# Input-gate products in four column groups, and modulation sums by transposes and a reduce

## The reference, cut to what matters

```
proj = xn @ w_in                          # (256, 1024) @ (1024, ...)
qk, v, o, i_pre, f_pre, u, sv, gates = split(proj)   # i_pre, f_pre: 4 columns each
i_pre + b_i, f_pre + b_f                  # input and forget gates of the 4 mLSTM heads
logf = log_sigmoid(f_pre); b = cumsum(logf); ...     # stabilised chunkwise mLSTM

ada   = silu(c)     @ w_ada + b_ada       # c, c_ctx: (1, 1024), w_ada: (1024, 6144)
ada_c = silu(c_ctx) @ w_ada + b_ada
sh1, sc1, g1, sh2, sc2, g2 = split(ada)   # shift, scale and gate vectors of 1024 each
```

## Time and profile before

| what | us |
|---|---|
| median of the timed runs | 1326.96 |
| lowest and highest of the three | 1324.94, 1327.00 |
| profiled execution, whole | 1323.78 |
| its span in the trace | 1322.1 |
| TensorE busy in it | 1289.8 |
| VectorE, ScalarE busy | 695.4, 501.6 |

### The profile page before, as it was taken

How to read it: one execution, slowest core, us unless ns; L and a number is a source line. 1 busy time by engine, 2 the same in 40 slices (tenths; PEclk the granted TensorE clock), 3 DMA queues, 4 the chain that set the end, 5 groups by cost and what they waited for, 6 DMA issues and landing times.

```text
span 1322.1 us, 18062 instructions
## 1 busy us (share of the span) xinstructions
PE 1289.8 (98%) x7214; PEld 908.7 (69%) x7214; DVE 695.4 (53%) x1174; ACT 501.6 (38%) x766; POOL 77.3 (6%) x83
## 2 busy tenths in 40 slices
PE   8999999999999999999999999999999999999998
PEld 7988887976775445444445444459956687799986
DVE  5675668666565222222322222257876877755552
ACT  5555574345242211111111111146414685744442
POOL 5740200100000000000000000000000000000000
PEclk9999999999999999999999999999999999999999
DMA  9653747958865999999999999995505334655540
GB/s 350 229 191 135 254 144 260 368 194 303 308 232 199 396 424 427 427 427 428 428 428 428 427 425 428 427 397 181 180 12 196 139 129 157 195 166 183 192 159 32
DMA packets 101349, 363.68 MB, mean 275 GB/s; under 512 B 4002, under 2 KB 28837, under 8 KB 88912
## 3 DMA queue, kind: packets, MB, share of 16 engines
q1 hardware_dynamic: 97792, 352.86, 68.7%
q0 software_dynamic: 3280, 9.58, 2.2%
q10 hardware_dynamic: 192, 0.06, 0.0%
HBM read 361.43 MB, written 1.05 MB: 274 GB/s over the span
## 4 chain that ended last, share of the span: by engine, by line
PE 84%; DVE 7%; ACT 4%; DMA 2%; issue 2%; ACTq 0%; DVEq 0%
PE bank L510 37%; PE bank L908 15%; PE bank L926 9%; PE bank L883 5%; PE bank L1253 5%; PE bank L939 2%; DVE ring_parts L1301 2%; DMA ring<-in_w 2%; PE bank L835 1%; PE bank L1056 1%; PE bank L916 1%; ACT ring_parts L2119 1%; PE bank L564 1%; DMA ring<-in_w_xkv 1%; PE bank L600 1%
## 5 line engine op out<-in xcount | busy, mean ns | idle before, releaser
L2119 ACT ACTIVATE ring_parts<-ring 128x1024 fp32r<-128x1024 f32 x234 | 242.6, 1057 | 231.5 <-PE bank L510 204.2
L1301 DVE TENSOR_TENSOR ring_parts<-ring,ring_parts 128x1024 fp32r<-128x1024 f32 x214 | 257.3, 1223 | 133.1 <-ACT ring_parts L2119 130.1
L510 PE MATMUL bank<-ring_parts,arena_parts 128*128 128x512 f32 x1056 | 271.7, 392 | 3.6 <-ACT ring_parts L2119 1.5
L510 PEld LDWEIGHTS bank<-ring_parts,arena_parts 128*128 128x128 f32 x1056 | 196.4, 188 | 48.7 <-ACT ring_parts L2119 2.9
L510 PE MATMUL bank<-arena_parts,ring_parts 128*128 128x256 f32 x1504 | 198.0, 284 | 1.2 <-DVE flank_parts L1307 0.7
L909 PE MATMUL bank<-ring,arena 128*64 128x512 f32 x448 | 197.9, 594 | 0.0
L908 PE MATMUL bank<-ring,arena 128*64 128x512 f32 x432 | 190.7, 594 | 6.1 <-issue 6.1
L510 PEld LDWEIGHTS bank<-arena_parts,ring_parts 128*128 128x128 f32 x1504 | 190.1, 192 | 2.1 <-DVE flank_parts L1307 0.8
L908 PEld LDWEIGHTS bank<-ring,arena 128*64 128x64 f32 x432 | 57.4, 137 | 125.3 <-issue 125.3
L510 PE MATMUL bank<-ring_parts 128*128 128x512 f32 (+1 forms) x624 | 117.2, 346 | 2.1 <-DVE ring_parts L1301 1.2
L926 PE MATMUL bank<-ring,arena 128*64 128x512 f32 x448 | 113.4, 595 | 1.1 <-DMA ring<-in_w 1.1
(11 more groups left out here) (385 smaller groups left out, 1440.0 us busy)
## 6 DMA issues: line engine op xcount, KB each, us to landing
ring<-in_w SPq DMA_DIRECT2D x83, 2048.0 KB, 20.4
ring<-in_w_in SPq DMA_DIRECT2D x27, 2048.0 KB, 9.4
flank<-in_w SPq DMA_DIRECT2D x13, 2048.0 KB, 20.7
ring<-in_w_ada SPq DMA_DIRECT2D x12, 2048.0 KB, 8.0
ring<-in_w_ffn_gate SPq DMA_DIRECT2D x11, 1024.0 KB, 5.4
ring<-in_w_ffn_up SPq DMA_DIRECT2D x11, 1024.0 KB, 8.0
ring<-in_w_ffn_down SPq DMA_DIRECT2D x5, 2048.0 KB, 7.9
ring<-in_w_xkv SPq DMA_DIRECT2D x4, 2048.0 KB, 16.3
```

The costliest lines, as they stand in the source:

```text
L510: mm = pe.matmul(ps[:, o:o + width], *pair, start=(o == 0 and kk == 0 and ha + hw == 0), stop=(kk == kn - 1 and (ha, hw) == terms[-1] and ...
L1301: dve.tensor_tensor(low, src, high, ALU.subtract).then_inc(low_ready, 1)
L2119: act.activation(high, src, ACT.Copy).then_inc(high_ready, 1)
```

## The change

Three edits are made, and what each engine issues changes as follows.

1. `iftok` has the weights as stationary operand: `wif` is padded with zeros from 8 to 32 columns, and contraction slice k goes to column group k % 4 with all 256 tokens streaming. That is 8 products [32 x 256] instead of 16 [128 x 8]. ScalarE copies [128, 256] instead of [128, 16]. A new memset on GpSimd writes the zeros before the transfer of `wif`.
2. `if` is two products of 4 columns of `pick` (now [128, 8]) with the copied parts, 256 columns each, instead of four transposes. They add the four parts and bring the rows to partitions 0 to 3.
3. `ada_sum` for the eight j that fill `adaT` turns the parts with four transposes [128 x 128]. VectorE then sums, in place of the product with `pick`, the four columns of each output in a reduce out of PSUM (L1463 after), followed by the bias addition from `adaT`. The sums of j = 4, 5, 10 and 11 stay.

```diff
-        wif = sb("wif", [P, KD, 2 * H])
+        wif = sb("wif", [P, KD, 32])
-        pick = sb("pick", [P, 2])
+        pick = sb("pick", [P, 2 * H])
+        if_parts = work[:, 384:384 + N]
...
                 if j == 0:
                     pe.wait_ge(s["silu_c"], 2)
-                    pe.wait_ge(s["pick_ready"], 1)
...
                     for c in range(4):
-                        mm = pe.matmul(ps[:, 2 * c:2 * c + 2], parts[:, c * P:(c + 1) * P], pick[:], start=True, stop=True)
+                        mm = pe.transpose(ps[:, c * P:(c + 1) * P], parts[:, c * P:(c + 1) * P], ident[:])
...
                     ps = take("iftok")
-                    for t in range(NT):
-                        for k in range(KD):
-                            mm = pe.matmul(ps[:, t * 2 * H:(t + 1) * 2 * H], actT[:, k, t * P:(t + 1) * P], wif[:, k, :],
-                                           start=(k == 0), stop=(k == KD - 1))
+                    pe.wait_ge(s["if_zeros"], 1)
+                    for k in range(KD):
+                        g = k % 4
+                        mm = pe.matmul(ps[32 * g:32 * g + 32, 0:N], wif[:, k, :], actT[:, k, :], start=(k < 4), stop=(k >= 4),
+                                       skip_group_check=True)
...
                     ps = take("if")
+                    pe.wait_ge(s["pick_ready"], 1)
                     for g in range(2):
-                        for t in range(NT):
-                            mm = pe.transpose(ps[0:H, g * N + t * P:g * N + (t + 1) * P],
-                                              stat[:, 8 + t * 2 * H + g * H:8 + t * 2 * H + (g + 1) * H], ident[:])
+                        mm = pe.matmul(ps[0:H, g * N:(g + 1) * N], pick[:, g * H:(g + 1) * H], if_parts, start=True, stop=True)
...
-                    did(dve.tensor_tensor(adaT[:, o:o + 4, :], ps[:, 0:8].rearrange("p (c n) -> p c n", n=2),
+                    did(dve.tensor_reduce(adaT[:, o:o + 4, :], ps[:].rearrange("p (c g r) -> p c r g", c=4, g=4)[:, :, 0:2, :], AX_X, ALU.add))
+                    did(dve.tensor_tensor(adaT[:, o:o + 4, :], adaT[:, o:o + 4, :],
                                           col2("b_ada_2")[:, b0:b0 + 4].unsqueeze(2).broadcast_to([P, 4, 2]), ALU.add), free(name))
...
-            did(act.activation(stat[:, 8:24], ps[:, 0:16], ACT.Copy), free("iftok"))
+            did(act.activation(if_parts, ps[:, 0:N], ACT.Copy), free("iftok"))
...
+            pool.memset(wif[:, :, 2 * H:], 0.0).then_inc(s["if_zeros"], 1)
-            pool.dma_start(wif[:], w["w_in"][0][:, 4096:4096 + 2 * H].rearrange("(k p) n -> p k n", p=P)).then_inc(s["misc_in"], 16)
+            pool.dma_start(wif[:, :, 0:2 * H], w["w_in"][0][:, 4096:4096 + 2 * H].rearrange("(k p) n -> p k n", p=P)).then_inc(s["misc_in"], 16)
```

More of the change, by code:

```diff
@@ L337, in two_blocks @@
         for name in ("E_ready G_ready O_rms On_ready SVn_ready Y_ready Z_ready a_ready choice_ready "
-                     "comb2_ready comb_ready consts count_ready gmoe_in ctx_in decay_cols dexp dmax down filt_arg "
+                     "comb2_ready comb_ready consts count_ready if_zeros gmoe_in ctx_in decay_cols dexp dmax down filt_arg "
                      "filt_in squared hid_ones fw3_in filt_sin gate_rows hF_ready h_rms if_ready lam_dot lam_exp lam_in mem_in "
@@ L1354, in _ @@
             dve.wait_ge(s["consts"], 9)
-            did(dve.tensor_reduce(pick[:], ident[:].rearrange("p (g r) -> p r g", g=4)[:, 0:2, :], AX_X, ALU.add), s["pick_ready"])
+            did(dve.tensor_reduce(pick[:], ident[:].rearrange("p (g r) -> p r g", g=4)[:, 0:2 * H, :], AX_X, ALU.add), s["pick_ready"])
             for t in range(NT):
```

## The result

The changed kernel took 1331.14 us (median of 7 runs, 1329.56 to 1331.85) against 1326.76 us for the kernel before on the same chip, a ratio of 1.0029 with an interval of 1.0018 to 1.0041. It is slower by 0.3%, where 1324.6 us was forecast, and outside the range. One of the seven runs of the kernel before took 2641.63 us and is not in the ratio; without it its median is 1326.11 us. The profiled execution took 1331.85 us with a span of 1330.1 us, 8.0 us above the span of the earlier trace rows.

What follows compares the result with a forecast made beforehand. The prediction took TensorE, busy 1289.8 of 1322.1 us, as the main bound, with VectorE or transfers pacing some stretches. Terms of -2.48, +0.42 and -0.34 gave -2.40, so 1326.96 became 1324.56 us; range 1321.8 to 1327.3.

Steps and rivals of the forecast that it cites:

- Gate product: Product for iftok between the third unit and its predecessors: 0.99 us in place of 3.47, term -2.48 (-2.54 to -1.62).
- gate turn: Behind the gate product, two float32 products replace four transposes: 0.86 us in place of 0.44, term +0.42 (0 to +0.64).
- sum 3: Modulation sum between xkv0 and the TensorE stretch behind it: 0.45 us in place of 0.79, term -0.34 (-0.35 to -0.20).
- Rival C: Column groups of the gate product don't overlap at 256 columns: +2.7 us, 1329.7 us; chance 0.07.
- The terms at nothing: Sums 0, 1, 2, 6 and 7 to 9, VectorE's reduces, ScalarE's copy, GpSimd's memset and the waits: each term 0.
- Sums 0 to 2 and 6: Sums ahead of the memory keys and xq0: savings covered by the transfer and VectorE, term 0.
- Rival A: All sums pay: seven more give 0.34 us each, -2.38 more, 1322.2 us; chance 0.10.
- No stall for a copy: Behind the gates, copies keep up with TensorE's 2.06 us lead; GpSimd's last quarter is ready 3.1 us early.
- rival B: Behind the gates, TensorE catches up with the copies and loses 2.06 us; -0.34 left, 1326.6 us; chance 0.13.
- Each such stretch begins with a TensorE event, so it moves along: Later stretches of ScalarE, VectorE and transfers in the chain shift with TensorE, so the 2.06 us gate lead lasts.
- three signs of being wrong: Gate product over 1.9 us; low-part wait between 40 and 90 us; experts' last transfer not moving by the front's gain.
- Sum: -2.48 + 0.42 - 0.34 = -2.40 us: Whole kernel: gate product, turn and one modulation sum added, other terms 0; bounds -3.0 and -1.2.

Runs made afterwards that it cites:

- e9: Kernel before with the new modulation sums alone, plus 64 padding instructions putting the jump back at its old place; 1327.00 us, ratio 0.9995 [0.9982, 1.0008].
- e5: Changed kernel with 133 fewer never-run instructions in the part the jump skips; 1323.63 us, ratio 0.9971.
- e6: Changed kernel with 96 padding instructions (two waits each) between long products of the value units; 1323.28 us against 1327.80, ratio 0.9968.
- e12: Changed kernel with 96 padding instructions between the value units' products, run a second time; 1321.65 us, ratio 0.9953.
- e10: Kernel before, unchanged, run once more for another profile; 1326.61 us in one run.
- e1: Changed kernel with some 96 more wait instructions at the start of TensorE's program, jump back at its old place; 1328.65 us, ratio 1.0018.

## Why the prediction was wrong

**Gate product, gate turn, sum 3: right.** The terms were 0.99, 0.86 and 0.45 us, and the chain after has 1.00, 0.96 and 0.44. The turn's 0.10 too little is all that was mis-sized among them; it lies inside the bounds. Rival C (column groups that don't overlap) fell with the 1.00 us: 16 rows at 0.06 each.

**The terms at nothing: right.** Sums 0 to 2 and 6 became idle time ahead of the transfer's and VectorE's end, the heads gained nothing, and the reduces' 0.19 us lay under cover. Rival A is refuted by the idle rows; e9's interval excludes it only just. Which of VectorE's rows ends the wait ahead of `xq0` stays open: the profile names L1307 before and after, the prediction took L1342. On the rule of the Trainium skill on transposes ("TensorE: Matmul & The Clock Gate", Part 4: PE-mode transpose) the measurement stands: four take 0.44 us, not the 1.10 estimated from that page.

**No stall for a copy: right.** The units behind the gates run nearly as before (L511 at 63.34 for 21.95 us), so rival B fell too. Of the 1.95 us that the gates gave, 1.54 were left at 86 us: the gate product started 0.13 us later than before, and the units behind it took 0.09 us more (96 rows) and 0.19 more (192 rows).

**"Each such stretch begins with a TensorE event, so it moves along": half right.** The lead was 1.67 us at the keys and 1.96 at 666 us. In the profile after it was lost between 666 us and the jump, on the wait and the clock at 675 us and on the last transfer, and in e5 at 850 us; in e6 and e12 it was there at the end, with spans of 1319.8 and 1319.5 us. The last expert transfer took 20.37 to 22.06 us in the chains that show it, so a single profile can't tell a lead of 2 us from its scatter. Of the prediction's three signs of being wrong the last one came: that transfer began 1.40 us earlier and ended 0.20 later. It isn't what cost the 8 us.

**"Sum: -2.48 + 0.42 - 0.34 = -2.40 us": the failed step.** The sum took only what the changed instructions do in their own places. It was right for them: without the stall the forecast span was 1319.7 us, and e6 and e12 measured 1319.8 and 1319.5 (e5, with its own late wait, 1323.4).
**The median.** The forecast put the same shift on the median. As it stands the change costs 4.4 us; with the jump repaired it gave more than forecast, 4.5 us in e6 and 7.1 in e12. That the rest is the clock's fall behind the old product, which the first profile of before lacked and e10's had, fits the count of profiles above, but no run shows how often the timed executions had it.

## What to carry to other kernels

Count where each taken jump and its target lie in the engine's instruction stream, before and after an edit, whenever code is skipped: 333 skipped instructions stalled or didn't by their place alone, 200 didn't where 333 did, and by the rule that fits all runs up to 256 never can (only the 200 was run). If a change leaves its own lines as forecast and the time moves elsewhere, look for a wait whose releaser is "issue" and put padding or a shorter jump against it before judging the change. "issue" alone is no proof: it stands at seven waits of L908 in each of the two kernels as well, and at 675 us one ended on a transfer. What marks a jump to missing code is the record of the jump itself (6.28 us in place of 0.48) and the block of instructions that moves only behind it. A few per mille between two versions of one kernel may be such a placement, so compare them with their jumps in the same place.

## What the runs showed of the hardware

- A jump to code that isn't fetched left TensorE idle for 5.76 to 5.88 us in four kernels with busy DMA queues and for 3.13 us with quiet ones. The granted clock was at half in or behind it, and the 48 rows that followed took 12.81 to 13.93 us in the four, in place of 11.17.
- 96 instructions that do nothing but wait (e1, e6) cost 5.6 us at the start of the program and nothing between 128 x 512 products.
- The clock can be at half behind a stretch in which TensorE was never idle by its rows: 32 rows of 8 columns, 3.47 us. It fell within 5 us of their start in six of eight profiles. Eight products in four column groups with 256 columns each, 1.00 us, were not followed by it in six profiles.
- Four column groups of 32 stationary columns run side by side at 256 streamed columns as well as at 512: 16 rows in 1.00 us against 1.85.
